# A decoder layer with 32 experts on one core: channel-major gates, 16 KB weight pieces, taps and a table load moved

## What is computed

```python
mod = silu(c) @ w_ada + b_ada                 # shift1, scale1, gate1, shift2, scale2, gate2
h = rms_norm(x, norm1_g) * (1 + scale1) + shift1
u_conv, q, k, v, g = split(h @ w_in)          # 7168 columns
y_conv = silu(layer_norm(depthwise_conv31(a * sigmoid(gt)) + conv_b)) @ w_conv_out + b_conv_out
y_attn = diff_attention(rope(rms_norm(q)), rope(rms_norm(k)), v) @ w_attn_out   # 8 heads, two maps each
g_conv, g_attn = split(sigmoid(g + b_gate))
x = x + gate1 * ((g_conv * y_conv + g_attn * y_attn) @ w_o)
h = rms_norm(x, norm2_g) * (1 + scale2) + shift2
logits = h @ w_router + b_router              # top 4 of 32, softmax over the chosen
for e in range(32):
    gu = h @ w_up[e] + b_up[e]                # 2048 columns, glu and lin interleaved
    act = glu * sigmoid(1.702 * glu) * (lin + 1)      # clamped
    y += combine[:, e] * (act @ w_down[e] + b_down[e])
x = x + gate2 * y
```

## Time and profile before

| | us |
|---|---|
| median of 3 runs (lowest, highest) | 1307.55 (1306.73, 1307.98) |
| the profiled execution | 1307.01 |
| its span in the trace | 1305.3 |
| TensorE busy in the span | 1119.2 |
| VectorE, ScalarE, GpSimd busy | 423.4, 218.2, 50.1 |
| mean rate of the DMA queues | 364 GB/s |

### The profile page before, as it was taken

The page is one execution under the profiler, slowest core; times in us unless marked ns, Lnnn a source line. Parts: engine busy times, 40 slices in busy tenths (PEclk is TensorE's granted clock), DMA queues, the critical chain, the costliest instruction groups (busy, mean ns, idle before and its releaser), DMA issues.

```text
span 1305.3 us, 18955 instructions
## 1 busy us (share of the span) xinstructions
PE 1119.2 (86%) x7716; PEld 436.1 (33%) x7716; DVE 423.4 (32%) x1142; ACT 218.2 (17%) x456; POOL 50.1 (4%) x83
## 2 busy tenths in 40 slices
PE   5999989999989666668999767988769696999996
PEld 4864344444433111113333112322213131333331
DVE  2379997651242111112232111222112121222231
ACT  1111023540122000001111100111001110111210
POOL 3010000055000000000000000000000000000000
PEclk9999989999999888889999788999889898999997
DMA  9997672347579999999999999999999999599997
GB/s 327 374 346 307 245 253 83 129 133 284 232 274 426 425 426 427 425 425 424 425 426 427 425 426 425 403 428 426 421 425 426 428 425 426 242 423 425 422 426 314
DMA packets 73739, 475.75 MB, mean 364 GB/s; under 512 B 6323, under 2 KB 18912, under 8 KB 38866
## 3 DMA queue, kind: packets, MB, share of 16 engines
q1 hardware_dynamic: 70324, 471.89, 88.5%
q0 software_dynamic: 816, 1.97, 0.6%
q10 hardware_dynamic: 2542, 1.06, 0.3%
HBM read 473.06 MB, written 1.05 MB: 363 GB/s over the span
## 4 chain that ended last, share of the span: by engine, by line
PE 46%; DMA 24%; SPq 17%; DVE 8%; ACT 3%; issue 1%; ACTq 0%; DVEq 0%
DMA weights<-in_w_down 19%; SPq L458 17%; PE bank L1549 15%; PE bank L1576 8%; PE bank L1281 6%; PE bank L1496 4%; DVE weights L863 4%; PE bank L1370 3%; DMA weights<-in_w_up 2%; PE bank L1429 2%; PE bank L1483 2%; DMA weights<-in_positions 2%; PE bank L1223 2%; PE bank L1503 1%; DMA weights<-in_w_ada 1%
## 5 line engine op out<-in xcount | busy, mean ns | idle before, releaser
L1549 PE MATMUL bank<-weights,buf_d 128*32 128x512 f32 x3008 | 390.8, 665 | 136.6 <-DMA weights<-in_w_up 136.6
L1549 PEld LDWEIGHTS bank<-weights,buf_d 128*32 128x32 f32 x3008 | 96.8, 116 | 407.2 <-DMA weights<-in_w_up 205.7
L1576 PE MATMUL bank<-weights,buf_d 128*32 128x512 f32 x1504 | 175.0, 598 | 13.3 <-DMA weights<-in_w_down 10.9
L1164 DVE TENSOR_SCALAR u_conv<-bank 128x256 f32<-128x256 f32 x47 | 20.0, 425 | 456.8 <-PE bank L1549 456.8
L774 ACT ACTIVATE u_conv<-u_conv 128x256 f32<-128x256 f32 x47 | 19.6, 416 | 668.2 <-DVE u_conv L1164 668.2
L1496 PE MATMUL bank<-buf_d 64*128 64x512 f32 x384 | 99.9, 640 | 0.9 <-DVE buf_d L1176 0.9
L863 DVE SCALAR_TENSOR_TENSOR weights<-u_conv,weights 128x256 f32<-128x256 f32 x240 | 97.5, 481 | 0.4
L1281 PE MATMUL bank<-weights,buf_d 128*128 128x512 f32 x192 | 84.7, 602 | 0.0
L1176 DVE TENSOR_TENSOR buf_d<-bank,u_conv 128x512 f32<-128x512 f32 x47 | 32.5, 692 | 148.2 <-PE bank L1576 148.2
L1576 PEld LDWEIGHTS bank<-weights,buf_d 128*32 128x32 f32 x1504 | 42.5, 109 | 111.3 <-issue 72.5
L774 ACT ACT_TABLE_LOAD x47 | 60.3, 1283 | 3.2 <-DVE u_conv L1134 2.4
(11 more groups left out here) (285 smaller groups left out, 844.5 us busy)
## 6 DMA issues: line engine op xcount, KB each, us to landing
weights<-in_w_up SPq DMA_DIRECT2D x128, 2048.0 KB, 34.3
weights<-in_w_down SPq DMA_DIRECT2D x64, 2048.0 KB, 37.2
weights<-in_w_in SPq DMA_DIRECT2D x10, 2048.0 KB, 14.1
weights<-in_w_ada SPq DMA_DIRECT2D x8, 2048.0 KB, 15.8
weights<-in_w_ada SPq DMA_DIRECT2D x8, 1024.0 KB, 11.9
weights<-in_w_in SPq DMA_DIRECT2D x8, 512.0 KB, 10.4
weights<-in_w_in SPq DMA_DIRECT2D x4, 1024.0 KB, 12.0
weights<-in_w_conv_out SPq DMA_DIRECT2D x2, 2048.0 KB, 7.9
```

The source lines that it names most:

```text
L1549: ins = t.matmul(UP[SLOTS * g:SLOTS * g + SLOTS, :], xgT[:, r, SLOTS * j:SLOTS * j + SLOTS], w[:, r, NB * g:NB * g + NB], start=False, sto ...
L1576: ins = t.matmul(DOWN[rows, :], actT[:, r, at:at + SLOTS], w[:, g, r, NB * i:NB * i + NB], start=(r == 1 and h == 0 and g == 0), stop=(h = ...
```

## The change

- Gates, `y_conv` and `y_attn` are computed channel-major: the weights are the stationary operand, 128 channels at a time, the 256 tokens the moving one, two such groups to a bank. The bias of the gates goes into ScalarE's copy, that of `y_conv` into VectorE's product, both from `cols`; the bias matmuls, their rows in six small loads, their GpSimd steps and masks go. The gated sum comes out transposed, so `mixT` and its copies go.
- A `w_down` chunk comes as one piece of 16 KB for each partition. Partition p then holds rows 4p to 4p+3, so the columns of `w_up` are taken in another order: the moving operand of the up matmuls, and the bias rows, are read as 4 elements in 8 (`up_group`).
- `mod2T` stands behind all four `value` projections. VectorE runs `conv(2, 17, 31)` and `conv(3, 0, 3)` ahead of its columns, `conv(3, 3, 11)` behind them, and ten taps each of pair 3 inside heads 0 and 1.
- The transposes of the small vectors and the zeroing matmuls stand ahead of `mod_row(0)`; two small loads join those that they wait for.
- In the routing: a Sqrt of one column on ScalarE between `keep_x1T(2)` and `square(1, 1)`, its result in `h_bias`, and a wait for it on VectorE ahead of line 1058; the copy into `place_s` on GpSimd; the loops of TensorE, ScalarE and SyncE start on `ends_ready`; the unit tables use the bank of `ends`.
- The right halves of the output are stored from ScalarE's queue.

The diff, cut to its core:

```diff
+        def up_group(flat, g):
+            return flat.rearrange("p (h c b q) -> p h b c q", h=2, b=2, q=4)[:, g // 2, g % 2, :, :]
-        order += [("ada", 1), ("v", 0), ("mod2T", 0), ("mod2T", 1)] + [("v", i) for i in range(1, 4)] + [("qkT", i) for i in range(8)]
+        order += [("ada", 1)] + [("v", i) for i in range(4)] + [("mod2T", 0), ("mod2T", 1)] + [("qkT", i) for i in range(8)]
...
-                    src = w_down[0, e, NB * (j - 4):NB * (j - 4) + NB, :].rearrange("(g p r) n -> p g (r n)", g=2, r=2)
-                    dst = wslot(e, j).rearrange("p (g n) -> p g n", g=2)
+                    src = w_down[0, e, NB * (j - 4):NB * (j - 4) + NB, :].rearrange("(p r) n -> p (r n)", r=4)
+                    dst = wslot(e, j)
...
-            sp.wait_ge(units_ready, 2)
+            sp.wait_ge(ends_ready, 1)
+            sp.wait_ge(units_full, 1)
             load_chunk(1, 4)
...
+            load(col_rows[40:56, :], b_gate[0].rearrange("(k p) -> k p", p=P), in_cols)
+            load(col_rows[56:64, :], b_conv_out[0].rearrange("(k p) -> k p", p=P), in_cols)
...
-                s.copy(gates[:, h % 2, NB * (h // 2):NB * (h // 2) + NB], bank(use)[:, :]).then_inc(bank_free[use % 4], 1)
+                s.activation(gates[:, 2 * h, :], bank(use)[:, 0:T], ACT.Identity, bias=cols[:, 40 + 2 * h:41 + 2 * h])
+                s.activation(gates[:, 2 * h + 1, :], bank(use)[:, T:2 * T], ACT.Identity,
+                             bias=cols[:, 41 + 2 * h:42 + 2 * h]).then_inc(bank_free[use % 4], 1)
...
             for i in range(3):
                 keep_x1T(i)
+            s.activation(h_bias[:, 0:1], eps[:], ACT.Sqrt).then_inc(warm, 1)
             square(1, 1)
...
+                act_e.wait_ge(out_right, tt + 1)
+                act_e.dma_start(out[0, tt * P:(tt + 1) * P, NB:D], x_tok[:, tt, NB:D]).then_inc(stored, 16)
...
             ada_row(1)
-            conv(2, 17, 26)
+            conv(2, 17, TAPS)
+            conv(3, 0, 3)
...
-            conv(2, 26, TAPS)
-            conv(3, 0, TAPS)
+            conv(3, 3, 11)
...
                 v.tensor_scalar(smax[:, par, :], smax[:, par, :], -(HD ** -0.5), None, ALU.mult).then_inc(s_max, 1)
+                if h < 2:
+                    conv(3, (11, 21)[h], (21, TAPS)[h])
...
+                for j in range(2):
+                    k = 2 * i + j
+                    ins = v.scalar_tensor_tensor(gates[:, k, :], bank(YC_USE[i])[:, T * j:T * j + T], cols[:, 56 + k:57 + k],
+                                                 gates[:, k, :], ALU.add, ALU.mult)
...
             for i in range(3):
                 add_branch(i // 2, i % 2)
             dve.wait_ge(h_sq, 3)
+            dve.wait_ge(warm, 1)
             v.tensor_scalar(h_bias[:], h_ss[:, 0, :], 1.0 / D, EPS, ALU.mult, ALU.add).then_inc(h_rms, 1)
...
+            def channels(use, n, c, j, rhs):
+                at = P * (2 * c + j)
+                for k in range(KD):
+                    ins = t.matmul(bank(use)[:, T * j:T * j + T], blk(n)[:, k, at:at + P], rhs[:, k, :],
+                                   start=(k == 0), stop=(k == KD - 1))
...
-                t.matmul(bank(gate_use(h))[:, :], bsel[:, h // 2, :], bias_b[:], start=True, stop=False)
-                for k in range(KD):
-                    if h and k == KD // 2:
-                        turn(h - 1)
-                    ins = t.matmul(bank(gate_use(h))[:, :], h1T[:, k, P * par:P * par + P], blk(n)[:, k, :],
-                                   start=False, stop=(k == KD - 1))
-                ins.then_inc(bank_full[gate_use(h) % 4], 1)
+                channels(gate_use(h), n, par, 0, h1T)
+                if h:
+                    turn(h - 1)
+                channels(gate_use(h), n, par, 1, h1T)
...
                 for k in range(KD):
+                    if i == 0 and k % 2 == 0:
+                        pe.wait_ge(mixed, k // 2 + 1)
                     ins = t.matmul(bank(use)[:, :], mixT[:, k, P * tt:P * tt + P], blk(n)[:, k, :],
...
                         for g in range(GROUPS):
                             ins = t.matmul(UP[SLOTS * g:SLOTS * g + SLOTS, :], xgT[:, r, SLOTS * j:SLOTS * j + SLOTS],
-                                           w[:, r, NB * g:NB * g + NB], start=False, stop=(j == 3 and r == 1))
+                                           up_group(w[:, r, :], g), start=False, stop=(j == 3 and r == 1))
```

More of the change, by code:

```diff
@@ L354, in build @@
         order += [("y_conv", i) for i in range(3)] + [("oT", i) for i in range(4)] + [("y_conv", 3)]
-        order += [(name, i) for name in ("y_attn", "mixT", "w_o") for i in range(4)]
+        order += [(name, i) for name in ("y_attn", "w_o") for i in range(4)]
         order += [("x1T", i) for i in range(4)]
-        order += [(name, 0) for name in ("lgT", "logits", "rank", "gather", "ends", "combT", "units")]
+        order += [(name, 0) for name in ("lgT", "logits", "rank", "gather", "ends", "combT")]
         use_of = {what: n for n, what in enumerate(order)}
@@ L371, in build @@
         X1T_USE = [use_of["x1T", i] for i in range(4)]
-        LGT_USE, LG_USE, RK_USE, GA_USE, END_USE, CT_USE, UN_USE = (
-            use_of[n, 0] for n in ("lgT", "logits", "rank", "gather", "ends", "combT", "units"))
+        LGT_USE, LG_USE, RK_USE, GA_USE, END_USE, CT_USE = (
+            use_of[n, 0] for n in ("lgT", "logits", "rank", "gather", "ends", "combT"))
+        units_bank, units_full = PS[END_USE % 4], sem("units_full")
         assert GA_USE % 4 == 1
@@ L1066, in _ @@
             step(v.reciprocal(rstd2, rstd2))
-            step(v.tensor_copy(place_s, iota_s))
+            dve.wait_ge(place_ready, 1)
             dve.wait_ge(b2_done, 1)
@@ L1229, in conv_rows @@
                         ins.then_inc(quarter_done, 1)
+            pe.wait_ge(made, 4)
+            for k in range(4):
+                t.matmul(PS[4 + k].rearrange("p (a c) -> p a c", a=4), identb[:],
+                         maskb[:, P:2 * P].unsqueeze(1).to_broadcast([P, 4, P]), start=True, stop=True, skip_group_check=True)
+            pe.wait_ge(in_cols, 16 * 11)
+            rest = TAPS * KD - P
+            t.transpose(PS[1][:, 0:P], convw_rows[:, 0, :], ident[:])
+            t.transpose(PS[1][:, P:P + rest], convw_rows[0:rest, 1, :], ident[0:rest, 0:rest])
+            t.transpose(PS[1][:, T:T + 64], col_rows[:, :], ident[0:64, 0:64])
+            for r in range(2):
+                ins = t.transpose(PS[1][:, T + 64 + 4 * r:T + 68 + 4 * r], norm2_rows.rearrange("p (c r) -> p r c", r=2)[:, r, :],
+                                  ident[0:4, 0:4])
+            ins.then_inc(vec_done, 1)
             pe.wait_ge(c_ready, 1)
@@ L1298, in value @@
                 proj(V_USE[i], h1T, i % 2, V0 + i // 2)
-            value(0)
+            for i in range(4):
+                value(i)
             for gi in range(2):
@@ L1309, in _ @@
                 ins.then_inc(bank_full[use % 4], 1)
-            for i in range(1, 4):
-                value(i)
             for i in range(8):
```

144 lines of the change are left out of this document (54 added, 90 removed).

## The result

| | before | after |
|---|---|---|
| median of four executions, us | 1307.61 (1306.73 to 1307.98) | 1299.72 (1299.34 to 1302.03) |
| profiled execution, us | 1307.01 | 1299.44 |
| its span, us | 1305.3 | 1297.7 |

The ratio is 0.9942, with a 95% interval of 0.993 to 0.9954: 7.6 us faster (0.6%; the medians differ by 7.9). 1297 was forecast, with a range of 1291 to 1304. The sum was to be 10.1 us; 7.6 came. Of the parts, the one in the mixer came out as forecast (3.3 to 3.9 us for 3.7), the one in the stream did not. I take them in the order of the prediction.

What follows compares the result with a forecast made beforehand. The prediction took the weight stream's start and rate, ten units at TensorE's pace and the transfers behind them as the bound: 1307.0 - 3.7 (start) - 6.1 (pieces) - 0.3 (stores) = 1296.9, predicted as 1297 us, range 1291 to 1304.

Steps and rivals of the forecast that it cites:

- First stage: Zeroing and small transposes move into TensorE's wait for w_ada; mod_col(0) starts at about 17.9 instead of 19.66, gaining 1.8 us.
- Modulation transposes: Behind all four values, TensorE's 6.19 us wait for ada_row(1) and the low clock go: 8.1 us gained.
- Taps: VectorE's convolution multiply-adds are late next; of 9.9 us gained on TensorE, 4.7 remain at head 1's channel sum.
- Channel-major: Projections behind the heads lose bias matmuls and the transposes of the gated sum: -2.9 us.
- Routing: Behind the last projection, VectorE's wait for the early Sqrt adds 4.1, low clock 0.8, earlier loops -0.5: +4.4 us.
- Rival 2: The routing wait costs nothing and the clock holds, giving 1292 us; 12% chance.
- Start: Start of the weight stream, after heads, projections and routing: 3.7 us earlier, with the 11th chunk issued near 374.
- Pieces: 16 KB pieces make each of 51 down chunks in the stream 0.12 us faster: -6.1 us.
- Rival 1: The larger pieces bring nothing, giving 1303 us; 13% chance.
- rival 4: The mixer gives nothing; if the pieces give half, 1305 us, no change that can be seen; 5% chance.
- Behind the ten units: In the run of ten units at TensorE's pace, faster down chunks gain nothing and only lengthen the stream's gap.
- Stores: Final output stores on two queues instead of one: last issue about 0.3 us earlier, -0.3 us.

Runs made afterwards that it cites:

- e6: Changed kernel with the modulation transposes back between value(0) and value(1): 1303.35 us, ratio 0.9963 to the kernel before.
- e8: Changed kernel with the early square root ahead of the three copies and pair 3's taps dealt 9, 6, 8, 8: 1290.77 us, ratio 0.9867.
- e10: Kernel before with only the modulation transposes moved behind the four values, taps left in place: 1316.82 us, ratio 1.0066.
- experiment 1: Changed kernel without the early square root and its wait (e1, 1293.55 us), or with the square root ahead of the copies (e2, 1293.75 us).
- e4: Changed kernel with w_down in 8 KB pieces and the up matmuls' moving operand contiguous again: 1306.32 us, ratio 0.999 to the kernel before.
- e9: Same kernel as e4, run a second time: 1305.75 us, ratio 0.9977 to the kernel before.
- e7: Kernel before with only 16 KB pieces of w_down and the new order of the up columns: 1304.05 us, ratio 0.9966.
- e1: Changed kernel without the early square root on ScalarE and without VectorE's wait for it: 1293.55 us, ratio 0.9886 to the kernel before.
- e5: The changed kernel itself, run again beside other runs: 1300.9 us, ratio 0.9943 to the kernel before.
- e2: Changed kernel with the early square root moved ahead of the three keep_x1T copies, wait kept: 1293.75 us, ratio 0.9894 to the kernel before.
- e11: e8 with ScalarE's eight small loads issued behind its first h1T activation instead of the fourth: 1295.9 us, ratio 0.9894 to the kernel before.

## Why the prediction was right, and where not

- **First stage, -1.8:** -2.0, 17.63 for 17.9; right.
- **Modulation transposes, -8.1:** right at the scores of head 0 (-8.65 with the order alone, -10.6 with the first stage). But the edit was worth only 2.4 us in the changed kernel (e6, median), because VectorE had become faster on its own. The step that failed is the time of the row: the sum had its 34 multiply-adds "end at 180.4 even if the row comes no earlier". The row came 6.84 us earlier, since I had followed neither the positions, which VectorE waits for (4.88 us), nor the rows of bias, which GpSimd no longer splits (2.9 us). It did no harm to the sum, as TensorE's columns held VectorE anyway; that is luck.
- **Taps, 4.7 of 9.9 us left:** right (209.00 for 209.5; heads -5.3 for -5.2), and e8 and e10 show the cause: with six of them in the idle time the heads end 4 us earlier, and with the order alone, without moving taps into the heads, the kernel is slower.
- **Channel-major, -2.9:** from the end of the heads to the end of the last projection it takes 84.47 us instead of 87.63, -3.2.
- **Routing, +4.4:** the wait was right, and it is the dearest single thing in the change: 5.5 to 6 us by experiment 1. The clock's part was 1.4 instead of 0.8; the earlier event took back 0.9 where I had 0.5. From the last projection to the 11th chunk it is 18.99 us instead of 14.42, +4.6 for +4.4. Rival 2 is out.
- **Start, -3.7:** 3.9 by the issue, 3.3 by the 20th chunk.
- **Pieces, -6.1:** the mis-sized term. 51 x 0.12 was read off a window of 6 us in one down chunk (414 GB/s), which is too short: in e4 and e9, whose pieces are 8 KB too, the same window reads 427 and 425, and after the change, where all pieces are alike, it reads 429 and the one of 13 us behind it 426. Over 88 chunks it is 0.069 us for each down chunk, 3.5 us for 51 of them. This is nearly all of what the forecast was off, 2.6 us. Rival 1 (nothing) is out by e7, and so is rival 4, whose mixer gives nothing.
- **Behind the ten units:** "those beside the ten units only lengthen the gap" is right: +1.2 us there. The delay of 1.7 us in slice 25 of the profile before, which I named and then left in the sum, had come from the clock in that one execution and didn't come again: -1.8. Neither is in the forecast, and that they nearly cancel in the comparison of the two profiles is luck.
- **Stores, -0.3:** from the start of the last four copies to the end of the span it is 5.2 us before and after. Counted from there the last issue ends 0.5 us sooner, and the span no sooner.

**The spread.** At least a part of the differences between executions of one kernel arises in the heads. Windows of 200 to 250 us, first the changed kernel, then its second profile, 3.6 us slower (the last three numbers are the granted clock, the DMA share and GB/s):

```profile
200.00:250.00 50.00, 42.54 (x234) 34.03 (x233) 36.51 (x78) 21.56 (x76) 0.00 (x0) 1.00 0.28 96
```

```profile
200.00:250.00 50.00, 43.57 (x219) 34.96 (x219) 35.12 (x73) 19.15 (x67) 0.00 (x0) 0.93 0.23 85
```

In the second the clock falls to the lower of its two levels (1.2 instead of 2.4 GHz) behind the wait for ScalarE that both have (3.34 and 3.33 us):

```profile
217.05 0.77 PE L1347 MATMUL bank<-weights 128*128 128x128 f32 x2 [3.33 <-ACT weights L671]
...
220.09 1.65 PE L1362 MATMUL bank<-weights 64*128 64x128 f32 x8
```

The eight small matmuls take 1.65 us where they take 0.93. From the end of the wait to the next step of the heads (L1337) it is 8.86 us instead of 6.01, so 2.9 of the 3.6 us come from the clock; the other 0.8 were there before the wait. The same wait is sometimes followed by the low clock and sometimes not: the low clock is there in the profiles of e1, e5 and e6, and not in those of the changed kernel, e2, e4 and e9. e1's profiled execution took 1297.5 us where its others took 1293.4 to 1293.7; in one of e2's, without a profile, the same distance appears (1297.4 over 1293.6 to 1293.8). In e8 that wait is 1.73 us, the clock stays up and the four executions lie within 2.3 us; in e11 it is 1.75 us, the clock stays up too, and five lie within 3.0. That the shorter wait keeps the clock up is no more than suggested by so few.

## What to carry to other kernels

When a stall goes, ask what the engine behind it had been doing in that time: a move that gains 8.65 us on TensorE made this kernel 8.9 us slower until VectorE's work was dealt out anew. The early table load was free here when it was put into the idle time of its own engine, ahead of work that depends on others (e2); behind that work, the wait for it put the whole chain behind it. And read a rate over many transfers (here 88), not over 6 us of one.

## What had not been expected of the hardware

- A load of half a KB that is issued 2.9 us later landed 13 us later (twelve profiles), and with eight small loads issued beside the weights the other queue took twice as long to issue two of its own (9.08 us for 4.43; one profile).
- VectorE's steps on 16 elements took up to 1.02 us instead of 0.17 beside GpSimd, and the long ones ended with its instructions.
- A matmul of 512 columns whose moving operand takes 4 of each 8 elements is as fast as one without gaps (667 ns), though the weight load of a transpose with a step of 2 costs 203 ns against 140.
- Pieces of 8 KB move 0.5% slower in this mix than pieces of 16 KB, and the kernels of either kind agree to within 0.05% (thirteen profiles).
- The wait of 3.3 us in the heads brings the lower clock in some executions and not in others, at 2.9 us in the one taken apart.
